# Computing some of the 128 key tiles as one 512-column product and one 256-column product

## The reference, cut to what matters

```
q = einsum('td,dhk->thk', x_t, w_q)              # queries; scores against sub_keys
sv, si = lax.top_k(s, K)                         # 16 of 128 keys, twice, for 8 heads
...
gate = jax.nn.softmax(fv, axis=-1)
u = u_emb[eidx]
act = jax.nn.gelu(jnp.einsum('thkd,td->thk', u, x_t), approximate=False)
return jnp.einsum('thk,thkd->td', gate * act, v)
```

## Time and profile before

| what | value |
|---|---|
| time, median of 3 runs | 2644.98 us (2639.59, 2644.98, 2645.97) |
| span of the profiled execution, first to last instruction | 2641.4 us |
| TensorE busy | 2431.8 us, 92% of the span |
| VectorE, ScalarE, GpSimd busy | 1854.0, 1319.5, 574.5 us |
| layer 0, Gelu of the first and of the last key tile start at | 232.15 and 599.84 us |
| layer 1, the same | 1257.96 and 1623.72 us |
| first instruction on ScalarE after each of these blocks starts at | 603.98 and 1628.08 us |

### The profile page before, as it was taken

How to read it: one execution, slowest core, us unless ns; L and a number is a source line. 1 busy time by engine, 2 the same in 40 slices (tenths; PEclk the granted TensorE clock), 3 DMA queues, 4 the chain that set the end, 5 groups by cost and what they waited for, 6 DMA issues and landing times. The chain is left out here.

```text
span 2641.4 us, 44330 instructions
## 1 busy us (share of the span) xinstructions
PE 2431.8 (92%) x16488; PEld 2160.9 (82%) x16488; DVE 1854.0 (70%) x3808; ACT 1319.5 (50%) x2022; POOL 574.5 (22%) x392
## 2 busy tenths in 40 slices
PE   5698999998999999778999999999999987888998
PEld 4488999997888887557999998888887866877877
DVE  6787888868777776775888865766666666654754
ACT  3345665556454545354665456545555535044643
POOL 0001666664000000200566666200000020000000
PEclk9799999999999999889999999999999998999999
DMA  8754777791777775724677774477674542042554
GB/s 348 279 165 149 181 183 181 182 260 56 247 264 262 266 265 192 275 80 144 171 182 182 182 183 123 135 216 216 218 218 155 175 140 80 4 129 95 174 167 153
DMA packets 200513, 480.52 MB, mean 182 GB/s; under 512 B 54448, under 2 KB 87728, under 8 KB 199760
## 3 DMA queue, kind: packets, MB, share of 16 engines
q1 hardware_dynamic: 150960, 431.75, 51.3%
q10 hardware_dynamic: 12576, 47.29, 4.8%
q0 software_dynamic: 36864, 0.15, 3.5%
HBM read 461.15 MB, written 17.96 MB: 181 GB/s over the span
## 5 line engine op out<-in xcount | busy, mean ns | idle before, releaser
L283 DVE TENSOR_TENSOR weight_low<-weight_raw,weight_high 128x1024 fp32r<-128x1024 f32 x732 | 893.6, 1223 | 375.2 <-ACT weight_high L277 365.1
L277 ACT ACTIVATE weight_high<-weight_raw 128x1024 fp32r<-128x1024 f32 x732 | 774.1, 1059 | 646.1 <-DMA weight_raw<-peer_v_dram 342.0
L387 PE MATMUL bank<-h_parts,weight_high 128*128 128x256 f32 x4608 | 842.7, 286 | 38.1 <-DVE h_parts L570 21.7
L387 PEld LDWEIGHTS bank<-h_parts,weight_high 128*128 128x128 f32 x4608 | 729.6, 195 | 40.3 <-issue 40.3
L387 PE MATMUL bank<-h_parts,weight_low 128*128 128x256 f32 x2304 | 657.8, 286 | 0.0
L1217 POOL DMA_INDIRECT gate_table<-pick_expo,pick_spot x256 | 475.3, 1857 | 594.4 <-DVE pick_expo L1319 379.9
L387 PEld LDWEIGHTS bank<-h_parts,weight_low 128*128 128x128 f32 x2304 | 448.6, 195 | 0.0
L394 PE MATMUL bank<-h_parts,weight_high 128*128 128x512 f32 x1120 | 400.5, 407 | 39.1 <-DVE weight_low L283 17.5
L1505 PE MATMUL bank<-weight_high,act_high 128*128 128x512 f32 x1024 | 316.0, 390 | 7.2 <-DVE act_low L1572 6.1
L1505 PE MATMUL bank<-weight_low,act_high 128*128 128x512 f32 x1024 | 315.3, 389 | 0.0
L1505 PE MATMUL bank<-weight_high,act_low 128*128 128x512 f32 x1024 | 315.2, 389 | 0.0
(11 more groups left out here) (350 smaller groups left out, 2594.3 us busy)
## 6 DMA issues: line engine op xcount, KB each, us to landing
weight_raw<-peer_u_dram SPq DMA_DIRECT2D x256, 512.0 KB
weight_raw<-peer_v_dram SPq DMA_DIRECT2D x256, 512.0 KB
kept<-ada_later_dram ACTq DMA_DIRECT2D x54, 512.0 KB
gate_table<-kept ACTq DMA_DIRECT2D x8, 2048.0 KB, 17.4
weight_raw<-peer_w_q_dram SPq DMA_DIRECT2D x32, 512.0 KB
kept<-gate_table SPq DMA_DIRECT2D x256, 64.0 KB, 3.4
weight_raw<-w_in_dram SPq DMA_DIRECT2D x32, 512.0 KB
weight_raw<-mlp_w_up_dram SPq DMA_DIRECT2D x32, 512.0 KB
```

What stands on the lines that cost most here:

```text
L277: self.nc.scalar.activation(self.high[:, slot, :], self.raw[:, slot, :], ACT.Identity) \
L283: eng.tensor_tensor(self.low[:, slot, :], self.raw[:, slot, :], self.high[:, slot, :].bitcast(F32), ALU.subtract) \
L387: mm = self.nc.tensor.matmul(out, w, x, start=(start and i == 0), stop=(stop and i == 2), skip_group_check=skip)
```

## The change

46 of the 128 key tiles of each layer are computed with `side_by_side`: tiles 3, 7, 11, ... 103 (26 tiles, the fourth of each four) and tiles 104 to 123 (20 tiles). Tiles 124 to 127 stay as they were. For such a "wide" tile m

- TensorE issues 8 products of 512 columns and 8 of 256 in place of 24 of 256;
- ScalarE, in place of the Gelu from the bank, copies the bank's columns 256 to 511 into `squares` (two buffers, by m % 2), and goes on with `weight_high` of tile m + 3;
- VectorE, right behind `weight_low` of tile m + 3, waits for that copy and adds the bank's columns 0 to 255 to it, into `acts`, and raises `halves_joined`;
- ScalarE, at the head of its list for tile m + 1, waits for `halves_joined` of tile m and takes the Gelu of `acts` in place;
- the bank counts as free for tile m + 4 once `halves_joined` has been raised.

TensorE's loop over 32 turns becomes four tiles written out, a loop of 25 turns, and 24 tiles written out.

```diff
@@ peer_scores: TensorE
+            def tile(turn, slot, wide):
+                core.wait_turn(pe, seg, turn, slot)
+                for c in range(KB):
+                    if wide:
+                        mm = core.side_by_side(core.bank[slot], slot, c, core.h_parts[:, c], c == 0, c == KB - 1)
+                    else:
                         mm = core.product(core.bank[slot][:, 0:T], slot, (core.h_high[:, c, :], core.h_low[:, c, :]), c,
                                           c == 0, c == KB - 1)
-                    mm.then_inc(used.sem, 1)
+                mm.then_inc(used.sem, 1)
...
+            for n in range(ALL_WIDE_FROM, P):
+                before = n - RING
+                if before in WIDE:
+                    pe.wait_ge(joined.sem, joined.at(WIDE.index(before) + 1))
+                else:
+                    pe.wait_ge(free.sem, free.at(NARROW.index(before) + 1))
+                tile(n // RING, n % RING, n in WIDE)
@@ peer_scores: ScalarE
             for n in range(P):
+                if n - 1 in WIDE:
+                    act.wait_ge(joined.sem, joined.at(WIDE.index(n - 1) + 1))
+                    nc.scalar.activation(acts[:, n - 1, :], acts[:, n - 1, :], ACT.Gelu)
                 act.wait_ge(used.sem, seg.first + RING + n + 1)
-                nc.scalar.activation(acts[:, n, :], core.bank[n % RING][:, 0:T], ACT.Gelu).then_inc(free.sem, 1)
+                if n in WIDE:
+                    nc.scalar.activation(low_half(n), core.bank[n % RING][:, T:2 * T], ACT.Identity).then_inc(copied.sem, 1)
+                else:
+                    nc.scalar.activation(acts[:, n, :], core.bank[n % RING][:, 0:T], ACT.Gelu).then_inc(free.sem, 1)
                 ahead = n + RING - 1
                 if ahead < P:
                     core.make_high(act, seg, ahead - ahead % RING, ahead % RING)
@@ peer_scores: VectorE
             for n in range(RING - 1, P):
                 core.make_low(dve, seg, n - n % RING, n % RING)
+                if n - RING + 1 in WIDE:
+                    m = n - RING + 1
+                    dve.wait_ge(copied.sem, copied.at(WIDE.index(m) + 1))
+                    nc.vector.tensor_tensor(acts[:, m, :], core.bank[m % RING][:, 0:T], low_half(m), ALU.add).then_inc(joined.sem, 1)
```

More of the change, by code:

```diff
@@ L1126 @@
 GATED_BY = 112
+ALL_WIDE_FROM = 104
+NARROW_FROM = P - RING
+WIDE = [n for n in range(NARROW_FROM) if n % RING == RING - 1 or n >= ALL_WIDE_FROM]
+NARROW = [n for n in range(P) if n not in WIDE]
 def picked_at(h):
@@ L1253, in peer_scores @@
     gate_at = {picked_at(h) + 4: h for h in range(HEADS)} | {GATED_BY: HEADS}
+    copied, joined = sig("halves_copied"), sig("halves_joined")
+    low_half = lambda n: core.squares[:, n % 2, :]
     with nc.Block() as block:
@@ L1263, in _ @@
         def _(pe):
[L1264 to L1269, removed]
+            def tile(turn, slot, wide):
[4 more added lines that the diff above has]
+                    else:
                         mm = core.product(core.bank[slot][:, 0:T], slot, (core.h_high[:, c, :], core.h_low[:, c, :]), c,
                                           c == 0, c == KB - 1)
-                    mm.then_inc(used.sem, 1)
+                mm.then_inc(used.sem, 1)
+            for slot in range(RING):
+                tile(0, slot, slot == RING - 1)
+            with pe.Fori(1, ALL_WIDE_FROM // RING) as turn:
+                for slot in range(RING):
+                    if slot < RING - 1:
+                        pe.wait_ge(free.sem, turn * (RING - 1) + free.at(slot + 2 - RING))
+                    else:
+                        pe.wait_ge(joined.sem, turn + joined.at(0))
+                    tile(turn, slot, slot == RING - 1)
+            for n in range(ALL_WIDE_FROM, P):
[5 more added lines that the diff above has]
+                tile(n // RING, n % RING, n in WIDE)
             pe.wait_ge(gated.sem, gated.at(HEADS + 1))
@@ L1333, in peer_scores @@
     exped.close(HEADS + 1)
-    free.close(P)
+    free.close(len(NARROW))
+    joined.close(len(WIDE))
+    copied.close(len(WIDE))
 WEIGHED_EARLY = 2
```

## The result

The changed kernel takes 2663.07 us (median of 4 runs, 2654.09 to 2664.07), the kernel before 2642.28 us (4 runs) beside it: a ratio of 1.0068, 95% interval 1.0048 to 1.0088, 13 to 23 us slower. The prediction was 2655 us, 10.2 us slower, range 2649 to 2666. The direction is right and the time lies in the range. But it is 8 us above the forecast time, and the difference to before, 20.8 us by the medians, is twice the forecast one. The experiments had to say why.

What follows compares the result with a forecast made beforehand. TensorE, busy 92% of the span, was taken as the bound. The terms -3.1 (tiles 3 to 103) + 0.6 (stage heads) + 7.4 + 6.1 (loops) - 0.8 (closing) gave +10.2 us, 2655.2 us, range 2649 to 2666.

Steps and rivals of the forecast that it cites:

- What TensorE gains: Key tiles made wide: 2.82 us in place of 2.88, saving 0.06 us each, at most 5.5 us in two layers.
- the small loss: Head of each key stage, where VectorE is the tighter engine: 0.3 us a layer lost.
- The loop: Tiles 104 to 123: ScalarE and VectorE wait for each other, 3.27 us a turn against TensorE's 2.82, bounds 3.15 and 3.45.
- Start, end, sum: Gelu of tile 127 starts 7.4 us later in layer 1, 6.1 us in layer 0; 0.4 us a layer comes back.
- Sum: Whole kernel: the key stages' differences, passed on in full, add up to +10.2 us.
- theory A: Follow-up runs' forecasts from the prediction's loop and wide-tile terms: +10.2 us for the change, -4.9 with the loop opened.
- tiles 3 to 103 stall as well: Rival: additions near the table loads cost 0.3 us at each of 52 wide tiles, 15.6 us more, 2671; chance 0.08.
- the clock falls: Rival: TensorE's pauses in tiles 104 to 123 lower its clock to a mean of 0.75, 20 us more, 2675; chance 0.04.
- The mechanism's own bounds: Tiles 104 to 123: a turn of 3.15 us gives a kernel time of 2650 us, one of 3.45 gives 2662.
- The loop doesn't bind: Rival: ScalarE comes round within 2.82 us in tiles 104 to 123, 5.5 us less, 2639.5; chance 0.07.
- binds by too little: Rival: a turn of 3.21 us or less in tiles 104 to 123, time 2653 or below; chance 0.25.

Runs made afterwards that it cites:

- e1: The kernel before, run again unchanged as a control: 2637.37 us, ratio 0.9992 against before.
- e11: The kernel before with one more product of zeros ahead of TensorE's loop in each key stage: 2640.22 us, ratio 1.0001 against before.
- e2: The change, with ScalarE's wait for the joined halves and their Gelu moved behind weight_high of tile m + 4: 2647.71 us, ratio 1.0023 against before.
- e7: The change, with VectorE's addition for tile m put ahead of weight_low of tile m + 3: 2646.62 us, ratio 1.0027 against before.
- e8: The change, with ScalarE's copy of the wide half made twice, the first to scratch: 2669.01 us, ratio 1.0109 against before.
- e5: The kernel before with TensorE's last 24 tiles of each key stage written out, nothing wide: 2658.75 us, ratio 1.0066 against before.
- e9: The kernel before with only layer 1's last 24 tiles written out, nothing wide: 2656.71 us, ratio 1.0070 against before.
- e10: The kernel before with 96 tiles of each layer written out, nothing wide: 2657.88 us, ratio 1.0060 against before.
- e12: The change with tiles 3, 7, ... 123 wide, TensorE looping 30 turns between four written-out tiles at each end: 2655.50 us, ratio 1.0049 against before.
- e6: e2 with tiles 104 to 123 in a loop of five TensorE turns instead of written out: 2642.78 us, ratio 1.0014 against before.

## Why the prediction was right, and what it lacked

**What TensorE gains.** 0.06 us a wide tile was right, and so was the small loss. The starts of `weight_low` are a poor mark for it, since each waits for a load and wanders by some tenths of a microsecond. ScalarE's first instruction on a tile's bank waits for TensorE itself. From the first Gelu to that instruction of tile 103, layer 1 took 1554.60 - 1257.96 = 296.64 us before, and the same in e1 and e11. The change has

```profile
1563.47 0.38 ACT L1309 ACTIVATE squares<-bank 128x256 f32<-128x256 f32 x1 [1.02 <-PE bank L394]
```

1563.47 - 1267.92 = 295.55, 1.1 us less (1.2 in layer 0), where 1.56 - 0.3 = 1.3 was forecast. e2 and e7 have 295.18 in layer 1, 1.5 us less. Why the change keeps a little less than those two wasn't asked by any run.

**The loop.** Right in its mechanism, place and size: 3.27 us a turn forecast, 3.264 and 3.269 measured. e2 and e7 open it at two different links and both restore 2.82 us with a TensorE that never waits; e8 lengthens one link by 0.26 us and the turn grows by 0.27. Two of the links were taken from neighbours, the Gelu's at 0.33 (it is 0.32) and the hop to ScalarE at 0.45 (it is 0.45).

**Start, end, sum.** Layer 0's block was to take 6.1 - 1.6 + 0.3 - 0.4 = 4.4 us more and takes 5.4; layer 1's 7.4 - 1.6 + 0.3 - 0.4 = 5.7 and takes 5.0. Together 10.2 by the sum, 10.4 measured against the first trace of before and 13.1 against e1.

**What failed is the step "Sum".** It lets the key stages' difference stand for the kernel's, "the rest is passed on in full", with no term for the stages that the diff leaves alone. They cost 10.4 us more in the profile. That number alone would prove little: outside the two blocks the spans of before, e1 and e11 are 1899.5, 1905.9 and 1893.2 us, and the change's is 1909.9. What bears it are the medians: the left-over column gives 8 to 19 us for each of the eleven kernels in which TensorE's tiles were written out or looped in another way, and nothing that can be told from zero in the two where they weren't (before again, and the one shifted by two instructions). For e5, e9 and e10, with nothing wide, this is a plain difference of two medians, 16 to 19 us. For the wide ones theory A's forecast is in it. So the price comes with another program and doesn't need the wide form; that it is the same price in all of them isn't shown.

Of the rivals, those that lie above the measured 2663 us, "tiles 3 to 103 stall as well" (2671) and "the clock falls" (2675), are both wrong: the trace shows those tiles faster and the clock at 1.00. The mechanism's own bounds, 2650 to 2662, miss the time. The range took it in because it had been widened for the spread of the runs. That the time fell inside is luck; that it is slower by more than the 0.3% isn't, since the blocks alone give 10.4 us.

**The rivals.** "The loop doesn't bind" and "binds by too little" fall with the pitch of 3.26. "The clock falls" didn't come about: the granted clock stayed at 1.00 (the 2.4 GHz level) through both stretches with a pause in front of every tile. The Trainium skill ("TensorE: Matmul & The Clock Gate", section "A second HAM failure mode: psum-queue depth-cycling") describes frequent short idle times of TensorE between groups of matmuls, in another kernel, as a cause of a swinging clock. The trace here doesn't show that: with a pause in front of every tile, 0.20 to 0.25 us in the rows, the clock held.

**What stays open.** Why a differently written program is slower. It isn't the amount of code (e5 against e10). In the second half of layer 0's peer block it isn't the place of the code behind the altered part either (e9). It isn't a shift by two instructions (e11). That half is where 4 to 13 us of it can be seen, as a rate of 250 to 257 GB/s in place of 260 or 261 and as slower packets in one queue. It isn't confined to that half, since the medians show more. The packets of instruction queue q8 over the whole kernel go from 49 to between 52 and 86 without the time following them. That the program's length moves where weights or code lie in memory would fit, but no run looked at that, and eleven against three is a correlation over few programs.

The granted clock is a rival that the record can answer. Between executions of one kernel the times spread by up to 23 us, and in the kernel before they go with the mean granted clock over the span: twelve executions at 0.970 took 2631.5 to 2641.6 us, three at 0.964 took 2642.8 to 2654.1. It doesn't explain the left-over. At 0.968 and 0.969 the change took 2664.1 and 2654.1 us and the kernel before, in 23 executions, 2635.8 to 2645.6. It does explain a part of e12's: its median clock is 0.963, before's 0.968. A straight line through the 66 executions of before that ran beside the experiments gives, as an estimate, 1.7 us for 0.001 of clock; by it the left-over of the eleven kernels is 7 to 14 us in place of 8 to 19.

**A version that beats both.** None. The late Gelu with loops (e6) beats the change by 0.0054 x 2640 = 14 us, and stands at 1.0014 [1.0000, 1.0028] against before: the 3 to 6 us that it gains in the key blocks (736.2 us in place of 742.0 and 739.2) are less than the 8 left over.

## What to carry to other kernels

When an instruction is added to two engines that already work in turns, write down the lists of both in order and look for a circle that closes within one item; its length is the sum of start-to-start distances, and no idle time in it counts as free. Opening it costs nothing but order: wait one item later, or put the addition ahead of what the partner waits for. And for a gain of a fifth of a per cent, first measure what an empty change of the program does (here 16 to 19 us in e5, e9 and e10, and nothing in e11), and compare the stretch that was changed in two traces, not only the two totals.

## What the runs showed of the hardware

- Writing out 24 or 96 tiles of a loop on TensorE, in one layer or both, with no other difference made the kernel 0.60% to 0.70% slower (e5, e9, e10). In e5 the key stages with the written-out code kept 288.5 and 72.1 us in layer 1, while the second half of layer 0's peer block, its own instructions the same, took 342.8 in place of 336.1 to 337.4 us.
- The stream of weights in the second half of layer 0's peer block ran at 260, 261 and 260 GB/s in before, e1 and e11, and at 250 to 257 GB/s in the other eleven, with 78 to 80% and 80 to 82% of the DMA engines' time busy. In one queue there a packet of 4096 bytes took on average 0.160 to 0.169 us in the three and 0.192 to 0.206 in the eleven.
- Over the kernel before's 66 executions the time went with the mean granted clock: 2631.5 to 2641.6 us at 0.970, 2642.8 to 2654.1 at 0.964.
- A 512-column product with its 256-column neighbour takes 2.82 / 8 = 0.353 us, three of 256 take 0.360: the wide form saves 2% of TensorE's time in this precision. The columns are the same 768; what goes is one of three weight loads.
